# The opening of a two-layer trunk: loads of the first two units re-ordered and cut into quarters, steps of 512 columns interleaved over both token tiles, and the first hidden tile turned by TensorE

## What is computed

```python
h = x
for i in range(DEPTH):                       # DEPTH = 2
    h = h + 0.5 * swiglu(rmsnorm(h, ffn1_norm[i]), ffn1_w_gate[i], ffn1_w_up[i], ffn1_w_down[i])
    z = rmsnorm(h, mix_norm[i]) @ w_in[i]    # conv heads and S5 heads share one projection
    y = concatenate([rmsnorm(y_a, conv_out_norm[i]), rmsnorm(y_s, ssm_out_norm[i])])
    h = h + y @ w_out[i]
    h = h + 0.5 * swiglu(rmsnorm(h, ffn2_norm[i]), ffn2_w_gate[i], ffn2_w_up[i], ffn2_w_down[i])
    h = h + (p[i] @ ple_w_proj[i]) * sigmoid(rmsnorm(h, ple_norm[i]) @ ple_w_gate[i])
return rmsnorm(h, final_norm)
def swiglu(u, w_gate, w_up, w_down):
    return (silu(u @ w_gate) * (u @ w_up)) @ w_down
```

## Time and profile before

| | us |
|---|---|
| median of 3 executions | 994.37 |
| the profiled execution's own time | 994.66 |
| its span, first to last instruction | 992.9 |
| TensorE matmul busy | 981.3 |
| VectorE busy | 871.5 |
| ScalarE busy | 515.8 |
| GpSimd busy | 365.7 |
| DMA, mean over the span | 183 GB/s |

### The profile page before, as it was taken

The page is one execution under the profiler, slowest core; times in us unless marked ns, Lnnn a source line. Parts: engine busy times, 40 slices in busy tenths (PEclk is TensorE's granted clock), DMA queues, the critical chain, the costliest instruction groups (busy, mean ns, idle before and its releaser), DMA issues.

```text
span 992.9 us, 16194 instructions
## 1 busy us (share of the span) xinstructions
PE 981.3 (99%) x5541; PEld 831.7 (84%) x5541; DVE 871.5 (88%) x1515; ACT 515.8 (52%) x763; POOL 365.7 (37%) x556
## 2 busy tenths in 40 slices
PE   9999999999999999999999999999999999999996
PEld 7888888899988888888878888889998888888885
DVE  7898999899889888998789978998998898787984
ACT  6544444584855444435564444445856454443463
POOL 6888999610137889960008500002002100000000
PEclk9999999999999999999999999999999999999999
DMA  9766565533646855564636555654544665655451
GB/s 278 223 211 204 177 208 172 171 128 129 211 143 210 244 176 205 169 212 170 213 127 212 186 194 171 210 174 134 160 171 148 202 213 174 207 184 196 169 191 43
DMA packets 143746, 181.65 MB, mean 183 GB/s; under 512 B 18448, under 2 KB 125648, under 8 KB 143696
## 3 DMA queue, kind: packets, MB, share of 16 engines
q1 hardware_dynamic: 142656, 179.68, 54.7%
q10 hardware_dynamic: 1040, 1.32, 0.4%
HBM read 179.93 MB, written 1.05 MB: 182 GB/s over the span
## 4 chain that ended last, share of the span: by engine, by line
PE 97%; ACT 1%; DVE 1%; ACTq 0%; issue 0%; POOLq 0%; POOL 0%; DVEq 0%
PE ps L1657 31%; PE ps L1659 30%; PE ps L1658 30%; PE ps L1672 1%; PE ps L1953 1%; PE ps L1919 1%; PE ps L1983 0%; PE ps L1977 0%; ACT bufB L674 0%; PE ps L1821 0%; DVE bufA L1263 0%; PE ps L1963 0%; ACT taps L688 0%; PE ps L1798 0%; PE ps L1991 0%
## 5 line engine op out<-in xcount | busy, mean ns | idle before, releaser
L892 DVE TENSOR_TENSOR wL<-raw,wH 128x1024 fp32r<-128x1024 f32 x334 | 426.2, 1323 | 18.4 <-ACT wH L480 17.1
L480 ACT ACTIVATE wH<-raw 128x1024 fp32r<-128x1024 f32 x334 | 335.4, 1052 | 99.5 <-PE ps L1659 92.0
L1657 PE MATMUL ps<-wH,uH 128*128 128x512 f32 x832 | 326.2, 392 | 2.4 <-DVE wL L892 1.3
L1659 PE MATMUL ps<-wH,uL 128*128 128x512 f32 x832 | 324.0, 389 | 0.0
L1658 PE MATMUL ps<-wL,uH 128*128 128x512 f32 x832 | 323.9, 389 | 0.0
L991 DVE STREAM_TRANSPOSE hTf<-bufB 32x128 f32<-32x128 f32 x640 | 193.6, 303 | 9.5
L1657 PEld LDWEIGHTS ps<-wH,uH 128*128 128x128 f32 x832 | 156.2, 188 | 36.8 <-DVE wL L892 2.4
L1659 PEld LDWEIGHTS ps<-wH,uL 128*128 128x128 f32 x832 | 156.2, 188 | 32.8
L1658 PEld LDWEIGHTS ps<-wL,uH 128*128 128x128 f32 x832 | 156.3, 188 | 31.6
L1657 PE MATMUL ps<-wH,hTH 128*128 128x512 f32 x352 | 138.0, 392 | 0.1
L1659 PE MATMUL ps<-wH,hTL 128*128 128x512 f32 x352 | 137.1, 389 | 0.0
(11 more groups left out here) (207 smaller groups left out, 1068.7 us busy)
## 6 DMA issues: line engine op xcount, KB each, us to landing
raw<-in_ffn_w_down_dram SPq DMA_DIRECT2D x88, 512.0 KB, 4.0
raw<-in_ffn_w_gate_dram SPq DMA_DIRECT2D x86, 512.0 KB, 4.0
raw<-in_ffn_w_up_dram SPq DMA_DIRECT2D x86, 512.0 KB, 5.0
raw<-in_w_in_dram SPq DMA_DIRECT2D x32, 512.0 KB, 4.4
raw<-in_w_out_dram SPq DMA_DIRECT2D x16, 512.0 KB, 3.8
raw<-in_ple_w_gate_dram SPq DMA_DIRECT2D x16, 512.0 KB, 4.3
raw<-in_glu_w_dram SPq DMA_DIRECT2D x4, 512.0 KB, 3.8
raw<-in_ple_w_proj_dram SPq DMA_DIRECT2D x4, 512.0 KB, 3.8
```

Source lines behind the costliest of these rows:

```text
L480: nc.scalar.activation(wH[:, slot, w], raw[:, slot, w], ACT.Copy).then_inc(wh_done, 1)
L892: nc.vector.tensor_tensor(wL[:, slot, w], raw[:, slot, w], wH[:, slot, w].bitcast(F32), ALU.subtract).then_inc((wl_half, wl_done)[a], 1)
L1657: mul(o, sH, vH, start=start, stop=False)
L1659: return mul(o, sL, vH, start=False, stop=stop)
```

## The change

Loads: unit 0 comes in four quarters, each with a semaphore of its own (`early_load`). ScalarE issues only the first norm vector, the up quarters 0 to 3, and, between quarters 0 and 1, x of tile 1 (first half). SyncE issues x of tile 0 (first half), the gate quarters 0 to 3, both second halves of x, all of unit 1 in halves, then unit 2, and only then 12 small vectors, then unit 3.

Order of work: the four transposes of x's tile 0 become plain float32 matmuls with the identity, six `warm` matmuls come before them and one after, none of the three that followed. ScalarE and VectorE split units 0 and 1 in steps of 512 columns, interleaved with x's scaling. TensorE interleaves both token tiles, and a step issues high by high first, as soon as `uH` and `wH` are there, then `uL` by `wH`, then high by `wL`. The turn of the small vectors moves from the end of unit 0 to the middle of unit 1's first half. One rounding of x (q = 3) moves from VectorE to ScalarE.

Chunk 0's hidden tile (layer 0, first feed-forward) is turned by `turn_hidden` on TensorE, put after the last matmul of unit 3; `hidden_H` and `hidden_L` read it in PSUM bank 6. VectorE's 16 block transposes for it are left out. Cut to its core:

```diff
@@ -293,6 +293,10 @@
 
             nth = (0, 2, 1, 3)[q] if l + m == 0 else q
             return l * 64 + 16 * m + 4 * nth + k + 1
+
+        def by_tensor(l, f, i):
...
@@ -316,18 +320,24 @@
             for dst, src in views[part]:
                 engine.dma_start(dst, src).then_inc(vec_ld, 16)
 
-        def unit0_quarters(engine, g, w):
-
-            dst = raw[:, 0, :].rearrange("p (k g c) -> p k g c", k=4, g=2)[:, :, g, :]
-            src = w[0, 0:4 * P, 0:FC].rearrange("(k p) c -> p k c", p=P)
-            engine.dma_start(dst[:, 0], src[:, 0]).then_inc(quarter_ld, 16)
-            engine.dma_start(dst[:, 1], src[:, 1]).then_inc(first_ld, 16)
-            engine.dma_start(dst[:, 2:4], src[:, 2:4]).then_inc(ld[0], 16)
+        def early_load(engine, n, g, k, done, width=1):
+
+            w = (ffn1_w_gate, ffn1_w_up)[g]
+            dst = raw[:, n, :].rearrange("p (k g c) -> p k g c", k=4, g=2)[:, k:k + width, g, :]
+            src = w[0, n * 4 * P:(n + 1) * 4 * P, 0:FC].rearrange("(k p) c -> p k c", p=P)[:, k:k + width, :]
+            engine.dma_start(dst, src).then_inc(done, 16)
 
         @block.sync
         def _(sp):
             sp.dma_start(xres[:, 0, 0:512], x[0, 0:P, 0:512]).then_inc(x_half_ld, 16)
-            unit0_quarters(sp, 0, ffn1_w_gate)
+            for k in range(3):
+                early_load(sp, 0, 0, k, quarter_ld[0][k])
+            early_load(sp, 0, 0, 3, ld[0])
+            for t in range(NT):
+                sp.dma_start(xres[:, t, 512:1024], x[0, t * P:(t + 1) * P, 512:1024]).then_inc(x_ld[t], 16)
+            for k in (0, 2):
+                for g in range(2):
+                    early_load(sp, 1, g, k, (quarter_ld[1] + [ld[1]])[k], 2)
...
@@ -361,19 +371,12 @@
                 for part in range(2):
                     slot = (base + part) % SLOTS
                     halves = gate_up(slot, wg, wu, 0, part)
-                    if l == 0 and base + part == 0:
-                        halves = []
-                    if l == 0 and base + part == 1:
-                        sp.dma_start(xres[:, 1, 0:512], x[0, P:2 * P, 0:512]).then_inc(x1_half_ld, 16)
-                        for dst, src in halves:
-                            sp.dma_start(dst[:, 0:2], src[:, 0:2]).then_inc(second_ld, 16)
-                        sp.wait_ge(consts, 1)
-                        vectors(sp, 0, slice(2, 13))
-                        halves = [(dst[:, 2:4], src[:, 2:4]) for dst, src in halves]
-                    unit(l, base + part, slot, halves)
-                if l == 0 and base == U_FFN1:
-                    sp.wait_ge(second_ld, 32)
+                    if l > 0 or base > 0:
+                        unit(l, base + part, slot, halves)
                 chunk(1, (0,))
+                if l + base == 0:
+                    sp.wait_ge(consts, 1)
+                    vectors(sp, 0, slice(1, NPV))
                 if then:
                     then()
                 chunk(1, (1,))
@@ -465,17 +468,11 @@
...
@@ -576,10 +574,11 @@
                 silu(l, f, i, unit_b, 1)
 
             def hidden_H(l, f, i):
+                src = ps[:, 6, :].rearrange("p (k n) -> p k n", k=2) if by_tensor(l, f, i) else hTf[:]
                 act.wait_ge(ht_turned, l * (2 * NFC) + i + (f * NFC + 1))
                 if not (isinstance(i, int) and i == 0):
                     act.wait_ge(wt_used, used(l, i * 3 + (FFN_BASE[f] + 1)))
-                nc.scalar.activation(hTH[:], hTf[:], ACT.Copy).then_inc(hh_done, 1)
+                nc.scalar.activation(hTH[:], src, ACT.Copy).then_inc(hh_done, 1)
 
             def last_hidden_H(l, f):
 
@@ -822,12 +821,11 @@
 
             def first_norm():
                 act.dma_start(pvec0[0:KD, :], vec(ffn1_norm, 0)).then_inc(vec0_ld, 16)
-                unit0_quarters(act, 1, ffn1_w_up)
-                act.dma_start(xres[:, 0, 512:1024], x[0, 0:P, 512:1024]).then_inc(x_ld[0], 16)
-                act.dma_start(xres[:, 1, 512:1024], x[0, P:2 * P, 512:1024]).then_inc(x_ld[1], 16)
-                act.wait_ge(consts, 1)
-                vectors(act, 0, slice(0, 2))
-                act.wait_ge(cleared, 1)
+                early_load(act, 0, 1, 0, quarter_ld[0][0])
+                act.dma_start(xres[:, 1, 0:512], x[0, P:2 * P, 0:512]).then_inc(x1_half_ld, 16)
+                for k in (1, 2):
+                    early_load(act, 0, 1, k, quarter_ld[0][k])
+                early_load(act, 0, 1, 3, ld[0])
 
                 def high(t, k):
 
@@ -838,19 +836,38 @@
...
-                act.wait_ge(wt_used, 1)
-                for k in range(4):
-                    high(0, k)
-                    if k < 3:
-                        act.wait_ge((quarter_ld, first_ld, ld[0])[k], 32)
+                act.wait_ge(wt_used, 2)
+
+                def weights(n, k):
+
+                    if k < len(quarter_ld[n]):
+                        act.wait_ge(quarter_ld[n][k], 32)
+                    else:
+                        act.wait_ge(ld[n], 32)
                     w = slice(512 * k, 512 * k + 512)
-                    nc.scalar.activation(wH[:, 0, w], raw[:, 0, w], ACT.Copy).then_inc(wh_done, 1)
...
-                split_at(0, 1, lambda: squares(0, 0, 0))
+                    nc.scalar.activation(wH[:, n, w], raw[:, n, w], ACT.Copy).then_inc(wh_done, 1)
+
+                high(0, 0)
+                weights(0, 0)
+                high(0, 1)
+                high(0, 2)
+                high(0, 3)
+                weights(0, 1)
+                high(1, 0)
+                high(1, 1)
+                weights(0, 2)
+                high(1, 2)
+                high(1, 3)
+                weights(0, 3)
+                act.wait_ge(cleared, 1)
+                squares(0, 0, 0)
+                weights(1, 0)
+                weights(1, 1)
+                squares(0, 0, 1)
+                norm_H(0, 0, 3)
+                weights(1, 2)
+                weights(1, 3)
                 vectors_turned(0, KD)
-                squares(0, 0, 1)
 
...
@@ -973,7 +999,8 @@
 
             def hidden_L(l, f, i):
                 dve.wait_ge(hh_done, l * (2 * NFC + 2) + i + (f * (NFC + 1) + 1))
-                nc.vector.tensor_tensor(hTL[:], hTf[:], hTH[:].bitcast(F32), ALU.subtract).then_inc(hl_done, 1)
+                src = ps[:, 6, :].rearrange("p (k n) -> p k n", k=2) if by_tensor(l, f, i) else hTf[:]
+                nc.vector.tensor_tensor(hTL[:], src, hTH[:].bitcast(F32), ALU.subtract).then_inc(hl_done, 1)
 
             def turn_Ei(l, s):
 
@@ -1006,7 +1033,8 @@
                     split_at(0, 3)
                 else:
                     hidden(l, f, 0, between)
-                turn_blocks(l, f, 0)
+                if not by_tensor(l, f, 0):
+                    turn_blocks(l, f, 0)
 
                 def turn_p(a):
                     dve.wait_ge(p_ld, (l + 1) * 16)
...
-                for k in range(4):
-                    low(0, k)
-                    w = slice(512 * k, 512 * k + 512)
-                    dve.wait_ge(wh_done, k + 1)
-                    nc.vector.tensor_tensor(wL[:, 0, w], raw[:, 0, w], wH[:, 0, w].bitcast(F32),
-                                            ALU.subtract).then_inc((wl_quarter, wl_half, wl_quarter, wl_done)[k], 1)
-                for k in range(4):
-                    low(1, k)
-                half_split(0, 1, 1, 0)
-                parts(0, 0, 1)
-                half_split(0, 1, 1, 1)
+                low(0, 0)
+                weights(0, 0)
+                low(0, 1)
+                low(0, 2)
+                low(0, 3)
+                weights(0, 1)
+                low(1, 0)
+                low(1, 1)
+                weights(0, 2)
+                low(1, 2)
+                low(1, 3)
+                weights(0, 3)
+                high_part(0, 0, 1)
+                low_part(0, 0, 1, 0)
+                low_part(0, 0, 1, 1)
+                weights(1, 0)
+                low_part(0, 0, 1, 2)
+                low_part(0, 0, 1, 3)
+                weights(1, 1)
                 parts(0, 0, 3)
+                weights(1, 2)
+                weights(1, 3)
 
             first_norm()
             for l in range(DEPTH):
...
@@ -1448,7 +1493,7 @@
             def spread_steps(l):
 
                 pool.wait_ge(pool_link, links[0])
-                pool.wait_ge(vec_ld, (l + 1) * (16 * NPV))
+                pool.wait_ge(vec_ld, (l + 1) * (16 * NPV) - 16)
                 g.tensor_copy(pvec[V_LDT:V_LDT + NB, :].rearrange("b (g p) -> b g p", g=2),
                               ldt[V_LDT:V_LDT + NB, :].unsqueeze(2).to_broadcast([NB, 2, ST])).then_inc(pv_full, 1)
 
...
+                    mul(ps[:, t, :], uL[at], wH[:, n, w], start=False, stop=False)
                     if k < 3:
-                        pe.wait_ge((wl_quarter, wl_half, wl_quarter)[k], (1, 1, 2)[k])
+                        pe.wait_ge((wl_quarter, wl_half, wl_quarter)[k], (2 * n + 1, n + 1, 2 * n + 2)[k])
                     else:
-                        take(0, 0)
-
```

(45 more changed lines are left out.)

64 lines of the change are left out of this document (37 added, 27 removed).

## The result

| | before | after |
|---|---|---|
| median, us | 994.73 (4 executions) | 1001.26 (4 executions, 999.49 to 1002.8) |
| ratio to before | | 1.0064, interval 1.0053 to 1.0076 |
| the profiled execution's own time | 994.66 | 1002.8 |
| its span | 992.9 | 1001.0 |
| first matmul of unit 2 | 21.25 | 24.73 |

The change costs 6.5 us where 3.9 were forecast, and 1001.26 lies 0.5 above the top of the range.

What follows compares the result with a forecast made beforehand. TensorE, busy 981.3 of 992.9 us, was taken as the bound. Opening 0.4 us lost, 0.4 allowed up to unit 3's end, and a 3.3 us hand-over put down 3.9 later: 994.4 + 3.9 = 998.3, range 996.0 to 1000.8.

Steps and rivals of the forecast that it cites:

- The small vectors: Their turn in unit 1: TensorE waits 1.0 us (0 to 2.7) for GpSimd's copy; unit 2 at 21.6.
- Opening: Up to unit 1: first matmul 1.3 us earlier, mostly lost again at quarter 1; unit 1 at 14.9, before 15.47.
- the upper bound (18.0): Latest landing of the last small vector, if the backlog holds SyncE up in issuing; 16.3 was expected.
- rival B: Small vectors land at 18 or later, held behind unit 2 in SyncE's queue: 1000.0 us and more; chance 0.13.
- Vectors in time: Case without a wait for the small vectors: unit 2 starts at 20.5, before 21.25.
- Unit 2 to unit 3's end: Stretch of 11.8 us, with 0.4 (0 to 0.7) allowed for closer work of ScalarE and VectorE; ends at 33.8.
- Hand-over: Hidden tile, unit 3 to down product: 3.3 us exposed on TensorE's path; down at 37.1, before 33.24.
- Rival C: Hand-over of the hidden tile is covered after all: 992.9 us with the opening's best; chance 0.04.
- small gain: Hand-over by the skill's rule alone, turning on TensorE: first down matmul at 33.24 - 0.2 + 0.45.
- rival D: TensorE's clock falls in the new 2.7 us idle stretch: 5.3 us at half pace cost 2.7, 1001.0; chance 0.06.

Runs made afterwards that it cites:

- e10: The e5 kernel with unit 0's quarter 1 ahead of x's second row tile on ScalarE's queue: 994.13 us, ratio 0.9992.
- e5: Changed kernel with the small vectors ahead of unit 2's loads and the four hidden transposes between unit 3's two tiles: 994.16 us, ratio 0.9996.
- b1: Kernel before with only the TensorE turn of the hidden tile added, behind unit 3's last matmul: 999.15 us, ratio 1.0041.
- e4: Changed kernel with the four hidden transposes between unit 3's two tiles, vectors as late as in the change: 997.46 us, ratio 1.0032.
- b2: Kernel before with only the TensorE turn of the hidden tile added, between unit 3's two tiles: 994.98 us, ratio 1.0000.
- e2: Changed kernel with the 12 small vectors issued ahead of unit 2's loads: 998.93 us, ratio 1.0035.
- e3: Changed kernel with the small vectors ahead of unit 2's loads and the hidden tile turned by VectorE again: 994.62 us, ratio 0.9999.
- e6: Changed kernel with 12 matmuls on `ones` ahead of the small vectors' turn: 1000.91 us, ratio 1.0059.
- e7: Changed kernel with 12 matmuls on `ones` behind the four hidden transposes, ahead of the first down matmul: 999.79 us, ratio 1.0053.
- e1: Changed kernel with the hidden tile turned by VectorE again, all else kept: 998.14 us, ratio 1.0031.

## Why the prediction was wrong in size

The direction and both places were as forecast. One term was too small (the small vectors), and one was left out of the sum (the clock).

- **Opening: as forecast.** First 512-column matmul at 6.05 (6.2 forecast), quarter 1 landed at 7.98 (8.0), second step 8.75 (8.8), unit 1 at 14.76 (14.9), the turn reached at 16.14 (16.25). The price of standing behind x in the queue was real: e10 takes it away. That the numbers met so well is luck in part. With the same order of issues the second step stood anywhere from 8.13 to 9.80 in nine traces. And the terms behind 8.8, as I listed them (4.77, twice 0.44, 0.9), make 15.35 and not 14.9; the matmuls, turns and restarts took 6.0 us instead of these 6.55.
- **The small vectors: the step that failed.** "The last vector is issued near 12.5" was 14.15, and this issue ended at 14.57. I had counted 13 large issues of about 0.46 each, which from SyncE's first issue at 0.73 makes 6.7; they ran until 8.50, 0.60 each, above all because those of unit 1 took 0.63 to 0.95 us. These 1.8 us are the whole miss of 1.65: from there to the last vector's issue it was 5.65 us, about what my 12.5 leaves for them, though 1.89 of it went to the first vector alone. I had put this hold-up of the queue only into the upper bound (18.0) and into rival B. The rest of the step: from the end of the issue to landing I had 3.7 us, and the copy started 3.9 after it; the copy took 0.29 instead of 0.82, so that TensorE went on 0.35 us after its start and not 1.05. The part on moved bytes did not set the time: at 15 to 16 us only 77 GB/s moved, so the large transfers were through 2.5 us before the copy. The wait was 2.5 instead of 1.0 us, unit 2 came at 24.73 instead of 21.6: 1.5 of this is the wait and 1.6 the clock.
- **Vectors in time: as forecast.** For that case I gave unit 2 at 20.5; e5 has 20.43.
- **Unit 2 to unit 3's end.** My allowance was 0.4: 24.73 to 36.88 is 12.15, against 11.8.
- **Hand-over: as forecast.** 3.24 us against 3.3, in the order that I gave, in after and in b1. Rival C (covered) is refuted where the transposes stand; between the tiles it holds (e4, e5, b2). The "small gain" that I gave for it is a slip: 33.24 - 0.2 + 0.45 is 0.25 later, not earlier.
- **The clock: the term that was left out.** I priced it as rival D with a chance of 0.06 and 2.7 us, for one stretch. In the profiled execution it falls at both, and costs 1.6 and 1.4. My argument against it, that 0.92 us idle had ended at the full pace, said nothing of 2.5 us. The rule that I weighed (the Trainium skill, "TensorE: Matmul & The Clock Gate", section "Why this matters for your kernels": gaps over about 3 us) would have made both stretches safe; the measurement decides, and here the clock fell at stretches of 2.51, 2.60, 2.63 (twice) and 2.64 us, and in b2 at 2.07.

With the measured wait (+1.5) and one fall (+1.4 to 1.6) the sum is 998.3 + 3.0 = 1001.3, the median of 1001.26. One fall and not two is an argument from the spans of after's four executions, 1001.0, 999.5, 999.4 and 997.7 us: the steps are of about one fall each, and only the first is traced, with two falls. The mean granted clocks (0.994, 0.995, 0.995, 0.998) agree, but they alone prove little, as executions of before have 0.995 to 0.999.

Rival B, with its chance of 0.13, is what came: the vectors were there after 18, and the time is over 1000.0. The top of the range was too low because B and D were each taken alone, though the late vectors of B open a second stretch in which the clock can fall.

What stays open: why the clock falls at a stretch of 2.5 us in one execution and not in the next; why e2's opening waits, each under 1 us, were followed by a fall, and those of e3 (0.74 and 0.84) were not; and why quarter 1 landed up to 1.7 us apart with the same order of issues, which decides what the new opening is worth.

## What to carry to other kernels

A transpose moved to TensorE is paid at its hand-over, not by its matmuls: put it where enough matmuls that don't need it stand behind it to cover the rounding and the subtraction (3.2 us here, 12 matmuls and some small turns), not as the last thing ahead of its consumer. When small transfers move behind large ones in a queue, count the hold-up of the issues themselves, and expect the data some 3.8 us after the last issue's end (3.3 to 4.3 here). An idle stretch of TensorE of 2.5 us costs its length and, in many executions, about 1.5 us more for the clock.

## What the runs showed of the hardware

- At stretches of 2.5 to 2.6 us of idle time the granted clock fell to the lower level in five of seven traced cases (after twice, e2, e6, e7) and stayed at 1.00 in two (e1, b1). At 2.07 us it fell in b2 and stayed in e4. Ahead of e1's stretch and of after's first one TensorE has the same instructions. In after the falls lasted for 3.7 and 3.0 us of matmuls.
- The pace of TensorE in the opening differs between executions as well: the four transposes of x at 4.27 took 1.06 us in before and b1 and 0.77 in b2, all with a clock of 1.00 in the windows.
- GpSimd's copy started 3.3 to 4.3 us after the end of the last small vector's issue in all thirteen traces (before 3.8, after 3.9, e6 3.3, b1 4.3), although that end lay anywhere from 8.8 to 14.9 us and other transfers stood ahead of it.
- One issue of a small vector took from 0.28 to 2.26 us. The long ones stand directly behind large loads: 1.87 to 2.26 in the six traces with the vectors behind unit 2, 0.41 to 0.74 in the four with them behind unit 1.
- Matmuls on `ones` in the gap lengthened nothing where they ended with the wait (e7) and cost 0.7 us where they ran past it (e6). The clock was at 1.00 behind both; that they keep it there is not shown by one trace each.
